# Fourteen of sixteen query-projection tiles computed from split operands

## The reference

```
h   = rms_norm(x, g_ffn)                       # 256 x 1024
qry = h @ w_q                                  # 1024 x 2048: 16 tiles of 128 columns
s1, s2 = qry . sub1, qry . sub2                # scores against 2 x 128 keys, 8 heads
top 16 of each side -> 256 sums -> top 16 -> expert numbers and gates
y   = sum over chosen experts of gelu(h . u[e]) * gate * v[e]
x   = x + y
```

## Time and profile before

| | |
|---|---|
| time, median of 3 | 2145.33 us |
| profiled execution, its own time | 2148.28 us |
| its span (first to last instruction) | 2146.5 us |
| mean granted TensorE clock | 0.986 |
| TensorE busy | 2046.2 us (95%) |
| VectorE busy | 1517.4 us (71%) |
| ScalarE busy | 1078.4 us (50%) |
| GpSimd busy | 209.0 us (10%) |

### The profile page before, as it was taken

One profiled execution on the slowest core, in us unless ns is written; L12 is line 12 of the kernel. 1 busy time (PEld: TensorE's weight loads), 2 busy tenths in 40 slices (PEclk: granted clock), 3 DMA queues, 4 the chain that ended last, 5 costly groups with the idle time before them and its releaser, 6 DMA issues.

```text
span 2146.5 us, 45873 instructions
## 1 busy us (share of the span) xinstructions
PE 2046.2 (95%) x15166; PEld 1921.3 (90%) x15166; DVE 1517.4 (71%) x3540; ACT 1078.4 (50%) x2199; POOL 209.0 (10%) x218
## 2 busy tenths in 40 slices
PE   8999999978999999999989999999998999999998
PEld 7758888968999999999988888899997878889997
DVE  5755499597677888888865377776665647777666
ACT  3241356796444444444455465554445555655454
POOL 0000199682000000000000000000000000000000
PEclk9989999999999999999999999999999999999999
DMA  7333555302558777778644533345553453345553
GB/s 298 120 125 129 218 164 166 128 0 85 182 185 301 281 271 280 275 277 280 212 138 158 180 134 110 134 162 179 185 178 119 166 177 109 102 156 176 182 179 108
DMA packets 103259, 376.11 MB, mean 175 GB/s; under 512 B 11472, under 2 KB 11744, under 8 KB 102880
## 3 DMA queue, kind: packets, MB, share of 16 engines
q1 hardware_dynamic: 88992, 323.86, 44.8%
q10 hardware_dynamic: 14144, 50.72, 6.0%
HBM read 373.47 MB, written 1.05 MB: 174 GB/s over the span
## 4 chain that ended last, share of the span: by engine, by line
PE 69%; issue 17%; DVE 6%; DVEq 4%; POOL 2%; ACT 2%; ACTq 0%; POOLq 0%
PE bank L747 20%; PE bank L753 20%; PE bank L750 20%; POOL part_lo L1502 2%; DVE one_hots L1767 2%; PE bank L936 1%; DVEq L2080 1%; PE bank L892 1%; PE bank L974 1%; DVEq L2092 1%; ACT part_hi L1183 1%; PE bank L856 1%; PE bank L862 1%; PE bank L859 1%; DVE arena L2081 1%
## 5 line engine op out<-in xcount | busy, mean ns | idle before, releaser
L1183 ACT ACTIVATE part_hi<-ring 128x512 fp32r<-128x512 f32 x1080 | 661.9, 626 | 429.3 <-PE bank L750 405.4
L1783 DVE TENSOR_TENSOR part_lo<-ring,part_hi 128x512 fp32r<-128x512 f32 x684 | 452.1, 689 | 219.6 <-ACT part_hi L1183 214.2
L747 PE MATMUL bank<-u_hi,part_hi 128*128 128x256 f32 (+1 forms) x1792 | 520.5, 290 | 30.3 <-POOL part_lo L1502 12.4
L753 PE MATMUL bank<-u_hi,part_lo 128*128 128x256 f32 (+1 forms) x1792 | 507.4, 283 | 0.0
L750 PE MATMUL bank<-u_lo,part_hi 128*128 128x256 f32 (+1 forms) x1792 | 505.7, 282 | 0.0
L747 PE MATMUL bank<-w_hi,part_hi 128*128 128x256 f32 x1376 | 390.6, 284 | 4.8 <-DVE w_lo L1810 3.3
L750 PE MATMUL bank<-w_lo,part_hi 128*128 128x256 f32 x1376 | 389.8, 283 | 0.0
L753 PE MATMUL bank<-w_hi,part_lo 128*128 128x256 f32 x1376 | 389.8, 283 | 0.0
L747 PEld LDWEIGHTS bank<-u_hi,part_hi 128*128 128x128 f32 (+1 forms) x1792 | 339.7, 190 | 40.5 <-POOL part_lo L1502 11.5
L753 PEld LDWEIGHTS bank<-u_hi,part_lo 128*128 128x128 f32 (+1 forms) x1792 | 342.2, 191 | 0.5
L750 PEld LDWEIGHTS bank<-u_lo,part_hi 128*128 128x128 f32 (+1 forms) x1792 | 340.5, 190 | 1.3
(11 more groups left out here) (277 smaller groups left out, 2982.5 us busy)
## 6 DMA issues: line engine op xcount, KB each, us to landing
ring<-stream_dram SPq DMA_DIRECT2D x606, 512.0 KB, 3.3
arena<-ada_dram ACTq DMA_DIRECT2D x96, 512.0 KB, 4.6
xT<-x_dram SPq DMA_DIRECT2D x4, 256.0 KB, 5.7
arena<-mem_dram SPq DMA_DIRECT2D x1, 1024.0 KB, 9.9
arena<-keys_dram SPq DMA_DIRECT2D x1, 1024.0 KB, 5.6
out_dram<-uT SPq DMA_DIRECT2D x2, 512.0 KB, 2.6
cst<-consts_dram SPq DMA_DIRECT2D x1, 841.0 KB, 14.8
cond<-cond_dram SPq DMA_DIRECT2D x1, 512.0 KB, 15.5
```

Of the source, the lines that this page charges most:

```text
L747: m = pe.matmul(o, hi, u(cc), start=first, stop=False, **flags)
L753: m = pe.matmul(o, lo, u(cc), start=False, stop=last, **flags)
L1183: act.activation(part_hi[:, h % 4, 0:width], ring[:, n % RING, (h % 2) * width:(h % 2 + 1) * width], ACT.Copy).then_inc(hi_ready, 1)
L1783: v.tensor_tensor(part_lo[:, h % 4, :], ring[:, n % RING, (h % 2) * 512:(h % 2 + 1) * 512], part_hi[:, h % 4, :], ALU.subtract).then_inc(l ...
```

## The change

The first two query tiles stay `linear`. The other fourteen become `passes` over 28 half slots. ScalarE makes the 28 high parts (three of them ahead of the normed chunks, one behind them, the others between evictions), and GpSimd all 28 low parts. The expert halves are numbered on from 28 (`PQ_HALVES`), so their buffers follow without a break: the high parts of expert halves 0 to 2 are made among the last evictions of the query tiles, that of half 3 after the evictions of the scores. `u_hi` is written chunk by chunk by ScalarE as the normed chunks come. `u_lo` is subtracted chunk by chunk on VectorE, after the two plain tiles have read `uT` (it overwrites it), and before the angles and the modulations in VectorE's stream. The sines and `fetch_early(2)` follow the eviction of tile 6, no longer of tile 8.

```diff
-PEER_HALVES = 2 * PEER_SLOTS
+PQ_PLAIN = 2
+PQ_HALVES = 2 * (PEER_Q - PQ_PLAIN)
+PEER_HALVES = PQ_HALVES + 2 * PEER_SLOTS
@@ TensorE
-            for j in range(PEER_Q):
-                linear(S_PQ + j, T_PQ + j, uT, DC, fresh=(p_normed, 0) if j == 0 else None)
+            for j in range(PEER_Q):
+                if j < PQ_PLAIN:
+                    linear(S_PQ + j, T_PQ + j, uT, DC, fresh=(p_normed, 0) if j == 0 else None)
+                    continue
+                b = free_bank(T_PQ + j)
+                for h in (2 * (j - PQ_PLAIN), 2 * (j - PQ_PLAIN) + 1):
+                    m = passes(h, 0, lambda c: (b[:, 0:S], c == 0, c == DC - 1),
+                               lambda c: u_hi[:, c, :], lambda c: u_lo[:, c, :],
+                               (plo_chunk, 0) if j == PQ_PLAIN else None)
+                m.then_inc(tile_full, 1)
...
-            pe.wait_ge(usplit_ready, 1)
@@ ScalarE
             root_of(root[:, 0:S], bank[0][:, 0:S]).then_inc(p_root, 1)
+            for h in range(3):
+                query_half(h)
+            for c in range(DC):
+                act.wait_ge(p_normed, c + 1)
+                act.activation(u_hi[:, c, :], uT[:, c, :], ACT.Copy).then_inc(phi_chunk, 1)
+            query_half(3)
             for j in range(PEER_Q):
+                if j >= 2:
+                    query_half(2 * j)
                 evict(T_PQ + j, qry[:, j, :])
-                if j == 8:
+                if 2 <= j < PEER_Q - 1:
+                    query_half(2 * j + 1)
+                if j == 6:
                     act.wait_ge(turn_ready, 1)
...
+            query_half(2 * PEER_Q - 1)
             act.drain().then_inc(gelu_done, 1)
-            high_parts(0, 0)
-            high_parts(1, 0)
@@ GpSimd
+            for h in range(PQ_HALVES):
+                low_half(S_PQ + PQ_PLAIN + h // 2, h, 0)
             with pool.Fori(0, (AHEAD - LAST_LOWS) // 6) as it:
@@ VectorE
             v.drain()
-            v.tensor_copy(u_hi[:, :, :], uT[:, :, :])
+            v.wait_ge(tile_full, T_PQ + PQ_PLAIN)
+            for c in range(DC):
+                v.wait_ge(phi_chunk, c + 1)
+                v.tensor_tensor(u_lo[:, c, :], uT[:, c, :], u_hi[:, c, :], ALU.subtract).then_inc(plo_chunk, 1)
             v.wait_ge(pos_loaded, 16)
...
             for n in range(8, 24):
                 modulation_early(n)
             v.drain()
-            v.wait_ge(tile_full, T_KEYS)
-            v.tensor_tensor(u_lo[:, :, :], uT[:, :, :], u_hi[:, :, :], ALU.subtract).then_inc(usplit_ready, 1)
```

More of the change, by code:

```diff
@@ L68 @@
     int(x) for x in np.cumsum([0, 2 * L_UQ, 48, 24, 16, 6 * FT]))
-assert all(h % 4 == 0 for h in (PEER_HALVES, LH_GATE, LH_WO, LH_OUT, LH_FFN, L_HALVES))
+assert all(h % 4 == 0 for h in (PQ_HALVES, PEER_HALVES, LH_GATE, LH_WO, LH_OUT, LH_FFN, L_HALVES))
 def slot_of_half(h):
@@ L409, in build @@
         lo_ready = sem("low_parts_ready")
-        usplit_ready = sem("normed_parts_ready")
+        phi_chunk = sem("mixed_normed_high_chunk_ready")
+        plo_chunk = sem("mixed_normed_low_chunk_ready")
         ada_used = sem("ada_used")
@@ L754, in passes @@
                 return m
+            for j in range(PEER_Q):
[8 more added lines that the diff above has]
+                m.then_inc(tile_full, 1)
+            pe.wait_ge(keys_loaded, 16)
+            pe.wait_ge(tile_out, T_KEYS)
+            for j in range(8):
+                tt, g0 = j // 4, (j % 4) * 4
+                b = free_bank(T_KEYS + j)
+                for g in range(4):
+                    side, h = (g0 + g) // 8, (g0 + g) % 8
+                    m = pe.matmul(b[:, g * P:(g + 1) * P], qry[:, 2 * h + side, tt * P:(tt + 1) * P],
+                                  keysT[:, g0 + g, :], start=True, stop=True)
+                m.then_inc(tile_full, 1)
             def expert_act(i, k, turns, slots=12):
@@ L761, in expert_act @@
                 for h in (2 * k, 2 * k + 1):
-                    m = passes(h, turns * (2 * slots), lambda c: (bank[i % 2][:, 0:S], c == 0, c == DC - 1),
+                    m = passes(h, turns * (2 * slots) + PQ_HALVES, lambda c: (bank[i % 2][:, 0:S], c == 0, c == DC - 1),
                                lambda c: u_hi[:, c, :], lambda c: u_lo[:, c, :])
@@ L769, in expert_sum @@
                 for h in (2 * k, 2 * k + 1):
-                    m = passes(h, turns * (2 * slots), lambda c: (bank[4 + c // 2][:, (c % 2) * S:(c % 2 + 1) * S],
+                    m = passes(h, turns * (2 * slots) + PQ_HALVES, lambda c: (bank[4 + c // 2][:, (c % 2) * S:(c % 2 + 1) * S],
                                                                     first and c % 2 == 0, False),
@@ L1158, in _, with split_half, split_slot, high_parts @@
                 square(sq[:, c, :], xT[:, c, :]).then_inc(p_sq, 1)
+            def split_half(n, h, uses, before, width=512):
+                act.wait_ge(loaded[n % RING], (uses + (n // RING + 1)) * 16)
+                if not isinstance(before, int) or before + h >= 4:
+                    act.wait_ge(half_begun, before + (h - 2))
+                act.activation(part_hi[:, h % 4, 0:width], ring[:, n % RING, (h % 2) * width:(h % 2 + 1) * width],
+                               ACT.Copy).then_inc(hi_ready, 1)
+            def split_slot(n, k, uses, before):
+                for h in (2 * k, 2 * k + 1):
+                    split_half(n, h, uses, before)
+            def high_parts(k, turns, slots=12):
+                split_slot(S_PEER + k, k, turns * (slots // RING), turns * (2 * slots) + PQ_HALVES)
+            def query_half(h):
+                n = S_PQ + PQ_PLAIN + h // 2
+                if h < PQ_HALVES:
+                    split_half(n, h, 0, 0)
+                else:
+                    split_half(n, h - PQ_HALVES, 0, PQ_HALVES)
             act.wait_ge(p_sum, 1)
             root_of(root[:, 0:S], bank[0][:, 0:S]).then_inc(p_root, 1)
+            for h in range(3):
[4 more added lines that the diff above has]
+            query_half(3)
             for j in range(PEER_Q):
+                if j >= 2:
+                    query_half(2 * j)
                 evict(T_PQ + j, qry[:, j, :])
-                if j == 8:
+                if 2 <= j < PEER_Q - 1:
+                    query_half(2 * j + 1)
+                if j == 6:
                     act.wait_ge(turn_ready, 1)
```

10 lines of the change are left out of this document (5 added, 5 removed).

## The result

The changed kernel takes 2161.93 us (median of 4 runs, 2160.37 to 2163.11), the kernel before, on the same chip, 2145.19 (4 runs, 2144.55 to 2149.36): ratio 1.0071, interval 1.0059 to 1.0084. It is 16.7 us slower, 7 more than predicted and 2 above the range. The direction and the long gap in TensorE came as predicted, the sum did not. The profiled execution took 2160.37 us.

A forecast was written before the change was run, and what follows sets the result against it. TensorE was taken to bound the kernel. Savings of 9.0 and 3.7 us against a 15.4 us stall, 1.7 clock, 6 modulations and small waits gave +11, taken as +10: 2155 us, range 2139 to 2160.

The forecast's parts named there:

- Savings: Query tiles and experts' start: fourteen tiles at 2.81 instead of 3.455 us save 9.0, experts' start 3.7 us.
- The wait before the first expert slot: Experts' start: TensorE's wait falls from 2.89 to 0.7 us, saving 2.2, with 1.5 us more from avoided half clock.
- The wait for the first `u_lo` chunk: Query tile 2: TensorE waits for VectorE's first subtracted chunk, 0.5 us lost.
- The moved wait: Behind query tile 6: ScalarE waits for VectorE's angles and modulations, TensorE stalls 15.4 us; ends 5.8 and 15.4.
- The second batch: Query halves 14 to 21: eight modulations collide with GpSimd's low parts, TensorE loses 6 us; bounds 0 and 9.2.
- The start: Start of query tiles: GpSimd keeps up with 0.1 us to spare, four halves ready by about 201; no cost.
- the last rival: Query tiles: normed chunks meet GpSimd's first halves, +1.2 us; DMAs and modulation rows late too: +15, 2160 us; chance 0.08.
- the last line of the sum: Whole kernel: the +10 us carried from profiled execution (2148.28 to 2158) to the median, 2145.33 + 10 = 2155 us.
- Modulations free: Query tiles: only the drained small instructions collide with GpSimd, modulations don't; +5, 2150 us; chance 0.17.
- Hardly any collision: Query tiles: VectorE and GpSimd hardly disturb each other, stall 5.8 us; -5, 2140.5 us; chance 0.17.
- The waits don't bite: Query tiles: ScalarE reaches its wait late enough or not at all, no stall; -12, 2133 us; chance 0.07.
- More is lost: Query tiles: normed chunks meet GpSimd's halves, ring DMAs and modulation rows land late together; +15, 2160 us; chance 0.08.

The follow-up runs named there:

- the fastest version: Changed kernel with high parts behind the chunks, modulations 8-15 in the residual sum, 16-23 under scores, fetch DMA issues spread, sines behind tile 10: 2137.04 us.

## Why the prediction was right or wrong

**Savings, right.** 2.83 us a tile (2.81 forecast). The wait before the first expert slot is 0.69 us (0.7), and the slot starts warm; done alone in the kernel before, this part brings 3.0 us. The wait for the first `u_lo` chunk is 0.61 us (0.5).

**The moved wait, right.** ScalarE waits behind tile 6 for VectorE, and TensorE stands for 15.98 us, 15.4 forecast, ended by GpSimd's low part. Ahead of it the angles collide at 1.24 to 1.46 us (1.45) ten times (ten); within it the modulations run free. The issues took 4.43 us, not 3.95, and half 14 1.65, not 1.30, since a modulation of the second batch ran beside it. Half clock behind the gap, 241 to 245: 15 records in 3.32 us, which at 0.117 would be 1.76, so 1.6 us (1.7).

**The second batch, half the forecast.** Modulations do collide with GpSimd (2.29 against 1.23 us), as forecast from L1742 and as "SBUF — State Buffer", section "Who interferes with whom", of the Trainium skill says of two-input instructions; no row of before had shown it for this one. But two of eight ran mostly while GpSimd stood, and part of the rest fell under the half clock. From the end of the gap to the last query tile TensorE takes 24.65 us (241.68 to 266.33); seven tiles at 2.83 are 19.8, the half clock 1.6, which leaves 3.2 us. The experiment that moves the batch away leaves 0.2 in the same sum (22.55 - 19.8 - 2.5). So it is 3 us, not 6: the term was mis-sized.

**The start, missed.** This is the step that failed: "GpSimd keeps up [...] and starts with four halves in hand (ready by about 201)" was priced at nothing. In the main sum the normed chunks pass beside GpSimd's first halves for free; only the last rival had 1.2 us for them. They took 2.0 us more, as two halves got in ahead of a chunk where I had allowed for one, and TensorE's first eviction came 2.9 us later against the root. Everything behind, angles and stall included, starts later. The 2.9 are two things. With the same 3.4 us at half clock, colliding chunks put the first eviction at 9.7 us and free ones at 8.4: 1.3 us, nearly the rival's 1.2. The rest is half clock in the plain tiles, 6.5 us of it here against 3.1 in the first trace of before, some 1.5 us. Five of the six traces with colliding chunks have 5.9 to 6.8 us of it and the sixth 3.4; the six with free chunks have 3.1 to 3.4 or none. So the longer half clock goes with the collision, but not in every execution, and why is not shown.

**Where the 6.9 us come from.** From the root the prediction has the experts at 274.4 - 190.91 = 83.5. Measured: 84.6 and 85.1. In the first trace: start +2.9, first `u_lo` chunk +0.1, fourteen halves ahead of the gap +0.3 (20.0 us, not 19.75), gap +0.6, the stretch behind it -2.75 (24.65 us against 19.7 + 1.7 + 6), together the +1.1 measured. The errors of the start and of the second batch nearly cancel; that is luck. The selection had 12.0 us of slack left at its end (13.4 before), so the delay passed on as forecast. Rounding 11 to 10 cost 1.0. So the profiled pair differs by 12.1 us, 2 more than forecast. The rest, 4.5 us, is between the profiles and the medians: the profiled execution of before stood 3 us above its median, 1.5 of it the half clock that its repeat lacks, and that of after 1.6 below its own. I carried the first offset over one to one to both kernels, and this conversion, the last line of the sum, is the second step that failed and the larger share of the miss. End against root, the two pairs of traces differ by 12.5 and 16.7 us, the medians by 16.7 both times. Of the 4.2 us between the pairs 1.5 are the half clock at the start of the first trace of before, 0.5 lies ahead of the experts of the changed kernel, and 2.1 lie behind the first expert slot, where the twelve traces differ by up to 4.3 us; what makes these 2.1 stays open.

**The rivals.** *Modulations free*: refuted, 2.29 us. *Hardly any collision*: refuted by the angles. *The waits don't bite*: refuted, but the fastest version is what that rival describes, with the waits taken off the path: 8.9 us gained of the 12.2 that I summed as the most. *More is lost*: nearest in its sum (2160 against 2161.93) and half right in its cause: the chunks did collide, while the modulation rows made VectorE wait only 4.8 us, most of it before GpSimd's restart.

## What to carry to other kernels

Before moving a feed for the busiest engine into another engine's stream, list every wait that already stands in that stream: one that was free for being early enough becomes a stall of the length of whatever it waits for, here 16 us against 9 us of savings. When an idle engine is put to work, check which instructions of its neighbour will now run beside it; price them one to one against its instructions, and move them to where it still rests, since taking one group away only lets the next one collide. And when the forecast is within 1% of the whole, compare landmarks of two executions of the kernel before, and the granted clock of each stretch beside them: one profile of it held 1.5 us of half clock that the other did not, and three of the gains above shrink by 1.7 to 1.9 us when the clock is taken into account.

## What the runs showed of the hardware

The same pause of TensorE (3.00 us before the plain tiles) was followed by half clock in one execution of the kernel before and not in the other, 1.5 us apart. Instructions of VectorE with one input collide with GpSimd as well: a `tensor_scalar` of 128 x 256 float32 takes 0.29 us alone and 1.22 to 1.34 beside it. Two-input instructions of VectorE without a drain between them also let GpSimd in: the eight normed chunks, back to back, lost 2.0 us to two of its halves. And beside VectorE's 1.23 us modulations GpSimd's half goes from 1.3 to about 2.3 us, alternating one to one (ten halves in 20.34 us with eight modulations among them, 14.00 without), so both engines fall to about half of their rate.
